# Running products of the forget gate, level by level, in the recurrent layers of a four-layer decoder

## What is computed

```python
proj = h @ w_in                       # q, f, i, g, 1024 columns each
q, v = silu(q), i                     # 8 heads of 128
log_f = logaddexp(log(lb), log1p(-lb) + log_sigmoid(f))
k = (1 - lb) * sigmoid(-f)
b = cumsum(log_f)                     # over the tokens of a chunk
attn[t, s] = sum_d q[t, d] * k[s, d] * exp(b[t, d] - b[s, d])     # s <= t
out = attn @ v  (+ the state that the earlier chunks left)
y = (rmsnorm(out) * silu(g)) @ w_out
```

## Time and profile before

| | us |
|---|---|
| median of 3 runs (1173.29 to 1173.63) | 1173.41 |
| the profiled execution, first to last instruction | 1172.2 |
| what the median is above that span | 1.2 |
| TensorE busy | 1162.8 |
| VectorE busy | 795.5 |
| ScalarE busy | 671.5 |
| GpSimd busy | 23.1 |
| TensorE from the end of the second group to the output projection, layer 0 (35.39 to 147.00) | 111.6 |
| the same in layer 3 (851.36 to 963.58) | 112.2 |

### The profile page before, as it was taken

How to read it: one execution, slowest core, us unless ns; L and a number is a source line. 1 busy time by engine, 2 the same in 40 slices (tenths; PEclk the granted TensorE clock), 3 DMA queues, 4 the chain that set the end, 5 groups by cost and what they waited for, 6 DMA issues and landing times.

```text
span 1172.2 us, 17197 instructions
## 1 busy us (share of the span) xinstructions
PE 1162.8 (99%) x6846; PEld 1030.6 (88%) x6846; DVE 795.5 (68%) x837; ACT 671.5 (57%) x797; POOL 23.1 (2%) x29
## 2 busy tenths in 40 slices
PE   9999999999999999999999999999999999999998
PEld 7999998888889989888888888888898999888886
DVE  6687777655656775756656875566888878665563
ACT  6965675444454545544546654455787566544443
POOL 1000000000001000000000000000000000000000
PEclk9999999999999999999999999999999999999999
DMA  9543335655466545654654646646543334654550
GB/s 342 185 144 108 109 108 190 234 186 176 182 218 170 177 140 166 211 197 163 211 198 146 219 175 215 215 144 214 179 124 129 108 109 144 198 200 177 184 192 36
DMA packets 86216, 202.92 MB, mean 173 GB/s; under 512 B 3357, under 2 KB 6503, under 8 KB 85904
## 3 DMA queue, kind: packets, MB, share of 16 engines
q1 hardware_dynamic: 86128, 202.10, 50.5%
q0 software_dynamic: 32, 0.03, 0.0%
HBM read 201.04 MB, written 1.08 MB: 172 GB/s over the span
## 4 chain that ended last, share of the span: by engine, by line
PE 93%; ACT 3%; DVE 2%; issue 1%; DMA 0%; POOL 0%; ACTq 0%; DVEq 0%
PE misc L619 10%; PE hb L619 10%; PE acc L671 10%; PE acc L672 10%; PE acc L673 10%; PE hb L624 5%; PE misc L624 5%; PE hb L565 4%; PE hb L566 4%; PE hb L563 4%; PE acc L843 2%; PE hb L580 2%; PE hb L578 2%; PE hb L579 2%; PE acc L831 1%; PE acc L832 1%
## 5 line engine op out<-in xcount | busy, mean ns | idle before, releaser
L1497 DVE TENSOR_TENSOR wlo<-raw,whi 128x2048 fp32r<-128x2048 f32 x184 | 416.7, 2292 | 139.8 <-ACT whi L1089 138.6
L1089 ACT ACTIVATE whi<-raw 128x2048 fp32r<-128x2048 f32 x183 | 342.6, 1905 | 121.3 <-PE acc L673 103.1
L671 PE MATMUL acc<-whi,arena_r 128*128 128x512 f32 x512 | 200.1, 391 | 0.0
L672 PE MATMUL acc<-wlo,arena_r 128*128 128x512 f32 x512 | 199.8, 390 | 0.0
L673 PE MATMUL acc<-whi,arena_r 128*128 128x512 f32 x512 | 199.5, 390 | 0.0
L619 PE MATMUL misc<-xhl,whi 128*128 128x512 f32 x512 | 122.7, 391 | 0.1
L619 PE MATMUL hb<-xhl,whi 128*128 128x512 f32 x512 | 122.7, 391 | 0.0
L673 PEld LDWEIGHTS acc<-whi,arena_r 128*128 128x128 f32 x512 | 96.2, 188 | 20.1
L671 PEld LDWEIGHTS acc<-whi,arena_r 128*128 128x128 f32 x512 | 96.2, 188 | 19.1
L619 PEld LDWEIGHTS misc<-xhl,whi 128*128 128x128 f32 x512 | 95.3, 188 | 20.0 <-DVE arena L1999 0.7
L672 PEld LDWEIGHTS acc<-wlo,arena_r 128*128 128x128 f32 x512 | 96.3, 188 | 18.8
(11 more groups left out here) (263 smaller groups left out, 1797.7 us busy)
## 6 DMA issues: line engine op xcount, KB each, us to landing
raw<-in_mlp_w_dram SPq DMA_DIRECT2D x128, 1024.0 KB, 5.4
raw<-in_a_w_in_dram SPq DMA_DIRECT2D x31, 1024.0 KB, 5.4
raw<-in_b_w_qkv_dram SPq DMA_DIRECT2D x12, 1024.0 KB, 7.2
raw<-in_a_w_out_dram SPq DMA_DIRECT2D x8, 1024.0 KB, 5.1
raw<-in_b_w_out_dram SPq DMA_DIRECT2D x4, 1024.0 KB, 5.0
arena<-in_x_dram SPq DMA_DIRECT2D x2, 512.0 KB, 5.3
raw<-in_a_w_in_dram SPq DMA_DIRECT2D x4, 256.0 KB, 5.3
arena<-in_decay_dram SPq DMA_DIRECT2D x1, 1024.0 KB, 12.1
```

Of the source, the lines that this page charges most:

```text
L671: pe.matmul(o, ys, h, start=first and kt == 0, stop=False, skip_group_check=True)
L672: pe.matmul(o, ys, l, start=False, stop=False, skip_group_check=True)
L1089: act.activation(whi[:, g % 2, u, 0:n], raw[:, g % 2, u, 0:n], ACT.Copy).then_inc(hi_done, 1)
L1497: dve.tensor_tensor(wlo[:, g % 2, u, 0:n], raw[:, g % 2, u, 0:n], whi[:, g % 2, u, 0:n].bitcast(F32), ALU.subtract).then_inc(lo_done, 1)
```

## The change

The decays are no longer sums of log f through TensorE with an exponential for each level. The gate f itself and k are computed by feature (f groups of kind "T", the order of the groups now f, q, f, q, i, g, each f and q group holding one quad). The levels go upward, from 1 token to 64. q times f and k are kept in place, and at each level VectorE multiplies half of q's tokens and half of k's tokens by the product of f over the neighbouring block (`operands`, `key_operands`). These block products are a tree that GpSimd computes, six steps for each quad. ScalarE copies the half of k that a level uses into a buffer (`k_pick`), while q is read by TensorE in place, with steps. The level steps begin in the third quarter behind the q group, and are spread over 24 quarters. The transposes of k, the decay matrix (1 MB) and the constant rows C0 and C1 are gone; the lower bounds are 16 more rows of `gain_rows`. In layer 3, f gets the lower bound by an addition of a column (`f_c`).

```diff
-LEVELS = [64, 32, 16, 8, 4, 2, 1]
+LEVELS = [1, 2, 4, 8, 16, 32, 64]
-            order = [2, 3, 0, 1, 4, 5, 6, 7]
+            order = [2, 0, 3, 1, 4, 5, 6, 7]
-        after_quarter = [(), (0, 1), (2, 3), (4,), (5,), (6, 7), (8,), (9,), (10, 11), (12,), (13,), (14, 15), (), (), (), ()]
+        after_quarter = {2: (0,), 3: (1,), 5: (2,), 6: (3,), 8: (4,), 9: (5,), 10: (6,), 11: (7, 8), 12: (9,), 13: (10,),
+                         14: (11,), 15: (12,), 16: (13,), 17: (14,), 18: (15,)}
...
+                        sp.dma_start(gain_rows[74:90, :], a_lower_bound.rearrange("l (f p) -> (l f) p", p=P))\
+                            .then_inc(const_in, 16)
+                        sp.dma_start(masks_in, c_mask).then_inc(masks_loaded, 16)
-                        sp.dma_start(decay_in, c_decay.rearrange("p a b -> p (a b)")).then_inc(decay_loaded, 16)
...
-                        group("W", g0, 0, acc_read, need, norm_steps(n), acc[0:2], early=True, half_used=unit_free)
-                        group("W", g0 + 1, 2, lambda k: None, need, banks=acc[2:4])
...
+                        group("T", g0, 0, acc_read, need, norm_steps(n), acc[0:2], early=True, half_used=unit_free)
+                        group("T", g0 + 1, 2, free, need)
...
                     def level_product(level):
...
+                        pe.wait_ge(p_done[level // 8], 8 * j + level % 8 + 1)
+                        quad, lev = divmod(level, 8)
+                        if lev == 7:
+                            pe.wait_ge(k_done, 14 * j + 7 * quad + 7)
+                        else:
+                            pe.wait_ge(k_sb, 14 * j + 7 * quad + lev + 1)
                         for h in range(4):
...
+                                pk = pick[lev % 2][:, h * P:(h + 1) * P]
+                                pq = halves(flat_qf, at, LEVELS[lev], True, P)
...
+                    also = {2: lambda: diagonal_products(0), 11: lambda: diagonal_products(1), 17: lambda: quad_outputs(0),
+                            20: lambda: (quad_outputs(1), oms_step(0), oms_step(1)),
+                            22: lambda: (oms_step(2), oms_step(3))}
...
+                    for c, kind in enumerate("TTWWTT"):
+                        group(kind, g0 + 2 + c, 4 + 2 * c, free, need, some_steps, early=c == 2)
```

ScalarE after the change:

```diff
+                    f_a(0)
+                    split_unit(g0 + 2, 0, free=j + 1)
+                    f_a(1)
+                    f_b(0)
+                    split_unit(g0 + 2, 1)
+                    f_b(1)
+                    silu_a(0)
                     silu_b(0)
...
+                    for quarter in range(24):
+                        if quarter == 0:
+                            silu_a(1)
+                        if quarter in (2, 4):
+                            f_a(1 + quarter // 2)
+                        if quarter in (6, 8):
+                            silu_a(quarter // 2 - 1)
+                        if quarter % 2 == 0 and quarter < 22:
+                            split_unit(g0 + 3 + quarter // 4, quarter // 2 % 2)
+                        if quarter == 0:
+                            silu_b(1)
+                        if quarter in (2, 4):
+                            f_b(1 + quarter // 2)
+                        if quarter in (6, 8):
+                            silu_b(quarter // 2 - 1)
+                        if quarter == 1:
+                            k_pick(0)
+                        if quarter == 10:
+                            k_pick(8)
+                        for level in after_quarter.get(quarter, ()):
+                            if level % 8 < 6:
+                                k_pick(level + 1)
+                        if quarter in (10, 11, 13, 15):
+                            v_copy(quarter // 2 - 4 - (quarter == 10))
```

VectorE after the change:

```diff
+                    def factors(quad):
...
+                        ch.did(dve.tensor_tensor(flat_qf[:, own], flat_q[:, own], hn_flat[:, own], ALU.mult), p_done[quad])
+                    def operands(level):
...
+                        dve.wait_ge(g_mm, 16 * j + level)
...
+                            ch.did(dve.tensor_tensor(q, q, other_totals(quad, m, True), ALU.mult), p_done[quad])
+                    def key_operands(level):
...
+                        dve.wait_ge(k_sb, 14 * j + 7 * quad + lev)
...
+                            ch.did(dve.tensor_tensor(k, k, other_totals(quad, m, False), ALU.mult), k_done)
...
+                    dve.wait_ge(rstd_ready, n + 1)
+                    f_a(0)
+                    f_a(1)
+                    split_unit(g0 + 2, 0)
+                    f_b(0)
+                    f_b(1)
+                    column(n)
+                    split_unit(g0 + 2, 1)
+                    if layer == 0:
+                        dve.wait_ge(gains_T, 2)
+                        ch.did(dve.tensor_copy(gains[:, 32:90], acc[2][:, 32:90]), gains_sb)
+                        ch.settle()
+                    f_c(0)
+                    f_c(1)
+                    silu_z(0)
+                    silu_a(0)
+                    silu_b(0)
+                    for quarter in range(24):
+                        if quarter == 0:
+                            silu_z(1)
+                        if quarter in (2, 4):
+                            f_a(1 + quarter // 2)
+                        if quarter in (6, 8):
+                            silu_z(quarter // 2 - 1)
+                        if quarter % 2 == 0 and quarter < 22:
+                            split_unit(g0 + 3 + quarter // 4, quarter // 2 % 2)
+                        if quarter == 0:
+                            silu_a(1)
+                            silu_b(1)
+                            factors(0)
+                        if quarter in (2, 4):
+                            f_b(1 + quarter // 2)
+                        if quarter in (3, 5):
+                            f_c(2 + quarter // 5)
+                        if quarter in (6, 8):
+                            silu_a(quarter // 2 - 1)
+                            silu_b(quarter // 2 - 1)
+                        if quarter == 9:
+                            factors(1)
+                        for level in after_quarter.get(quarter, ()):
                             if level == 8:
                                 part_tiles(0)
                             if level % 8 != 7:
+                                key_operands(level + 1)
+                                operands(level + 1)
                                 select(level)
-                            if level + 2 < 16:
-                                operands(level + 2)
+                        if quarter == 4:
                             diagonals(0)
```

Here `f_a(b)` evacuates a bank of f (VectorE) and takes ln(1 + exp) of it (ScalarE), `f_b(b)` is two VectorE steps and then the exponentials that make f and k, and `silu_z(b)` evacuates a bank of q. TensorE may start the bank after next only when that has been done. GpSimd's part:

```diff
+                        for m in LEVELS[:6]:
...
+                            ch.did(pool.tensor_tensor(to[:, there:there + count // 2], pairs[:, :, 0], pairs[:, :, 1],
+                                                      ALU.mult), tree_ready if m == 32 else None)
```

More of the change, by code:

```diff
@@ L43, in decay_sums @@
 def decay_sums():
[L48 to L57, removed]
+    return np.zeros((1, 1), np.float32)
 def level_masks():
@@ L181, in build_decoder @@
         ones = sb("ones", [P, P])
-        gains = sb("gains", [P, 74])
-        decay = sb("decay", [P, 16, P], F32R)
+        gains = sb("gains", [P, 90])
+        tree = sb("tree", [P, 2, 1008])
+        pick0 = sb("pick", [P, 512])
+        bounds = sb("bounds", [P, 5, HEADS])
         masks = sb("masks", [P, 10, P], U8)
@@ L338, in free_count @@
         def free_count(layer):
-            return {0: 0, 1: 12, 3: 24}[layer]
+            return {0: 0, 1: 14, 3: 26}[layer]
         def used(g):
@@ new lines, in bank_of, with scaled, f_a @@
+                    def bank_of(region, b):
+                        h = 2 * (b % 2)
+                        return region[:, b // 2, :, h:h + 2, :].rearrange("p t h x -> p h t x")
+                    def scaled(out, bank):
+                        return dve.tensor_tensor(out, over_banks(bank),
+                                                 rstd[:, :].rearrange("p (h t x) -> p h t x", h=1, t=TT)
+                                                 .to_broadcast([P, 2, TT, P]), ALU.mult)
+                    def f_a(b):
+                        k = (0, 1, 4, 5)[b]
+                        dve.wait_ge(bank_ready, b0 + k + 1)
+                        out = scratch[b % 2][1].rearrange("p (t h x) -> p h t x", h=2, t=TT)
+                        if b < 2:
+                            ch.did(scaled(out, acc[b][:, :]), f_z)
+                        else:
+                            ch.did(scaled(out, hb[b % 2][:, :]), bank_free, free_count(layer) + k - 1)
@@ L1639, in gate_b, with f_c @@
[L1639 to L1647 removed]
+                        turn(dve.tensor_tensor(k, f, z, ALU.subtract))
+                    def f_c(b):
+                        if layer == 3:
+                            dve.wait_ge(fk_done, 4 * j + b + 1)
+                            for h in range(2):
```

(17 more changed lines are left out.)

544 lines of the change are left out of this document (176 added, 368 removed).

## The result

The changed kernel takes **1213.9 us** (median of 4 runs, 1213.17 to 1214.86) against 1173.35 for the one before (4 runs, 1173.21 to 1173.63): ratio 1.0345, 95% interval 1.033 to 1.036, slower by 40.5 us. The profiled execution took 1213.17 us, with a span of 1211.0; before, the span was 1172.2.

The account below looks back on a forecast made before the run. TensorE bound the kernel before; afterwards it would wait for the serial ScalarE-VectorE chain. Span 1172.2 + 20.0 (layer 0) + 20.1 (layer 3) = 1212.3, plus 1.2 to the median: 1213.5 us, range 1192 to 1236.

Parts of the forecast that it names:

- the walk: Step-by-step times of ScalarE's and VectorE's queues in layer 0, giving TensorE's releases and waits; layer 0 grows by 20.0 us.
- What TensorE loses: Recurrent layers: decay sums and transposes gone, 17.0 us removed per layer; less added feature-major work, 31.9 us in both.
- the two links of 1.9 and 2.0 us: Even quarters 0 to 8: ScalarE's split (1.9) and ln(1+exp) (2.0), which VectorE's split waits for.
- The last step: Layer 0 after level 5's release at 101.6: 63.5 us more, to 165.1, with quarters and level steps nearly even.
- the tree: GpSimd's second-quad products delay VectorE's key(3) and query(3): 1.9 us per recurrent layer, at most 2.1 each.
- the finest operands: VectorE's key and query operands before level 1's product in layer 0, counted at 1.6 us together.
- Step 3: Layer 0, from factors to level 1's operands: 11.1 us, to 64.8; TensorE waits 5.7 for level 1.
- the last term: 1.2 us added to the span of 1212.3, as the median of the runs lies above the profiled span.
- rival C: TensorE at half clock after its waits in quarters 0 to 10: +8 us per layer, 1229, up to 1237; chance 0.14.
- The stepped operand: Products streaming q with steps: taken as nothing, at most 0.8 us per product, 6 us per layer, +12 for the range.
- A: Quarters 0 to 9 of both recurrent layers: queues keep up, TensorE stays the bound, 1141.5 us; chance 0.07.
- B: Waits there but shorter, half of them through better overlapped handovers: 1177 up to 1192 us; chance 0.09.

Follow-up runs that it names:

- e9: Changed kernel with ScalarE's splits ahead of ln(1+exp), also at layer start, levels spread over quarters 2 to 19, first quad's diagonals in quarter 13: 1161.87 us, ratio to before 0.9902.
- e1: Changed kernel with ScalarE's split put ahead of ln(1 + exp) in quarters 0, 2, 4, 6 and 8: 1177.43 us, ratio to before 1.0029.
- e5: Changed kernel with GpSimd's tree of the second quad held back until the query operands of level 4 are through: 1211.87 us.
- e7: e1 with splits first and silu_z(0) earlier at layer start, plus level steps ahead of the gate in quarters 2, 6 and 8: 1170.68 us.
- e3: Changed kernel with matmuls nobody reads put ahead of TensorE's waits, 16.3 us per recurrent layer at full pace: 1212.73 us.
- e4: Changed kernel with the level products' moving operand read in one stretch instead of in steps (output differs): 1214.1 us.

## Why the prediction was right

The forecast was 1213.5 us and slower; 1213.9 came out, and the mechanism is the one in the walk. Point by point:

- **What TensorE loses.** Right in kind: the decay sums and the transposes are gone. How much that is worth shows in e9, where TensorE waits least: 1137.2 us busy against 1162.8. That is 25.6 less where the sum had 31.9. An estimate closes most of it: e9's mean granted clock was 0.996, half pace for some 9 us, which is 4 to 5 us of busy time, and four products took 0.38 more each. The change as made could not use it, because of the order of the other queues.
- **The walk through layer 0.** The six releases of TensorE were worked out as 40.6, 53.7, 64.8, 79.1, 90.4 and 101.6; they came at 39.58, 52.47, 64.28, 79.91, 91.01 and 102.11. Releasers were those named: silu before the diagonals, query operands before each level. At the first one the record names the copy of gains, but that had ended at 38.75; the evacuation that I named ended at 39.48, 0.1 before TensorE began. Three of the releases and, first, VectorE's cast of the masks, from which the walk began:

```profile
24.36 0.82 DVE L1511 CAST masks<-arena 128x1280 uint8<-128x1280 f32 x1
...
52.47 2.02 PE L841 MATMUL misc<-arena 128*128 128x128 f32 x16 [1.68 <-DVE arena L1600]
...
79.91 2.05 PE L832 MATMUL acc<-arena 128*128 128x128 f32 x8 [2.92 <-DVE arena L1645]
...
102.11 2.04 PE L832 MATMUL acc<-arena 128*128 128x128 f32 x8 [5.13 <-DVE arena L1645]
```

  The last step (63.5 us) took 63.8. The longest wait was not before level 5, as I had said (5.1), but before level 1 (5.6). e1 shows that this was the cause and not only the order of events: the two links of 1.9 and 2.0 us that the walk had in each stage, taken out, gave 36.5 of 39 us.
- **A term too large: the tree.** I took 1.9 us per layer and e5 shows 1.0. I had added a whole first and second GpSimd step, but the first was already 0.1 us on its way and took 1.04 rather than 1.3, and the second held up its operand by only 0.23.
- **A term too small: the finest operands.** The operands of the finest level, which multiply by f itself with single elements, take 1.13 us each; both together took 2.45 us from 61.83 to the release where I counted 1.6. Step 3 took 11.8 in place of 11.1 for it. The groups of the changed kernel:

```profile
L1645 DVE TENSOR_TENSOR arena<-arena,tree 128x512 f32<-128x512 f32 x20 | 14.3, 715 | 2.6 <-PE acc L832 0.6
L1645 DVE TENSOR_TENSOR arena<-arena,hn 128x512 f32<-128x512 f32 x4 | 4.6, 1150 | 2.1 <-PE acc L832 1.8
```

  With the tree's 0.9 the other way it nearly cancels.
- **Luck in the start and in the last term.** The first release came 1.0 us early, and so did the cast of the masks, 24.36 where it was 25.34. Seen from the cast, the release is as worked out (15.2 us behind it), and layer 0 grew by 19.9 for a forecast of +20.0; seen from the start of the program, by 18.9. The late start belongs to single executions: in the profiled execution of e7 the cast stands at 25.22, in those of the changed kernel and of all other experiments between 24.28 and 24.55. So the profiled execution of the kernel before was a long one: 1172.2 us of span, where most of its executions on record have 1171.3 to 1171.8. Every execution lies 1.8 to 2.3 us above its own span, and the 1.2 that I added was the median less the span of that long one. The span after was 1.3 below the sum, and the median lies 2.9 above it. The two nearly cancel, so the agreement to 0.4 us is luck; the mechanism is good to about 1 us per layer.
- **Size of the waits.** Forecast some 35 us of idle time per recurrent layer, 22 came. Some 8 of the 13 are rival C's mechanism, half pace behind each long wait, as e3 shows with its 30 us of slack; the other 5 stay open. I had the right argument for it (the next wait swallows it) but expected it either not to occur or to cost 8 per layer; it occurred, and taking it away behind most of the waits gave 1.2 us in both layers together (e3).
- **The stepped operand** at nothing: right in the time (e4), with 0.38 us for each product of single elements, inside the bound of 0.8.
- **Rivals.** A (TensorE stays the bound) fell as worked out: it needed stages of 5.8 to 7 us, and they were 11.1. With the splits first they are 7.6, and even e9 is 20 us above A's 1141.5. B (half the waits) fell. C gave the symptom, not the cost: the products of levels 1, 3 and 5 did take 1.7 us to the next matmul, which I had named as a sign of being wrong (1.6 us), and the time was still that of the walk. It was no good sign, since C's pace can be there without C's cost.

## What to carry to other kernels

When a change takes work from the engine that is the bound, walk the queues of the others step by step at its new pace: their busy share said nothing here (68% and 57%), the place of one instruction per quarter in one queue was worth 36 us. In a loop where two engines hand data back and forth, put work that waits for neither (a weight split) ahead of the chain on the engine that feeds it, and let the other engine's share of it cover the chain. And an engine's waits in a profile are a lower bound of its slack, if it ran slower after them. The slow stretch is swallowed as long as another wait follows; behind the last one it can cost (1.4 us in e1's layer 3).

## What the runs showed of the hardware

- Behind the waits of 4.2, 5.6, 2.9 and 5.1 us TensorE's granted clock was 0.50: 0.21 us per matmul of 256 columns in place of 0.12, 1.7 us per level product in place of 0.8 to 0.9. Where the wait was filled with other matmuls it was 1.00. Behind waits of 3 us it was the one or the other: 0.50 at 902.10 in e1, behind 3.03 us, and 1.00 at 83.80 in e1, behind 3.19.
- A moving fp32 operand read as single elements with steps costs TensorE 0.38 us on 0.81 per eight matmuls; in runs of two 0.06; in longer runs nothing.
- A GpSimd step on SBUF held up a VectorE step with two inputs in SBUF (1.48 for 0.69 us) and left those that read PSUM alone (0.73 and 0.67). It goes the other way too: GpSimd's own first tree step took 1.04 us by itself and 2.18 at 37.35, beside a split of VectorE.
